# Four-quadrant products in the RWKV inverse with a loop on TensorE, and paired rope products in attention

## What is computed

```
S = S * w_t + (S a_t) b_t^T + v_t k_t^T ;  y_t = S r_t        # a = -kk, b = kk * a
y = (y - mean) * rsqrt(var + 64e-5) * ln_w + ln_b              # per head
```

```
s = (q . k) * 192**-0.5 ; s = where(kpos <= qpos, s, min) ; p = softmax(s) ; o = p v
```

## Time and profile before

| | us |
|---|---|
| median of 3 runs | 2612.54 (2611.12 to 2614.38) |
| the profiled execution's own time | 2613.09 |
| its span, first to last instruction | 2611.3 |
| PE busy | 2537.2 (97%) |
| DVE busy | 1269.4 (49%) |
| ACT busy | 862.6 (33%) |
| POOL busy | 1181.0 (45%) |

### The profile page before, as it was taken

One profiled execution on the slowest core, in us unless ns is written; L12 is line 12 of the kernel. 1 busy time (PEld: TensorE's weight loads), 2 busy tenths in 40 slices (PEclk: granted clock), 3 DMA queues, 4 the chain that ended last, 5 costly groups with the idle time before them and its releaser, 6 DMA issues.

```text
span 2611.3 us, 36164 instructions
## 1 busy us (share of the span) xinstructions
PE 2537.2 (97%) x13941; PEld 1953.8 (75%) x13941; DVE 1269.4 (49%) x1579; ACT 862.6 (33%) x1168; POOL 1181.0 (45%) x583
## 2 busy tenths in 40 slices
PE   8999999899999998889999999999999999999999
PEld 6676777688888776777788887888887446788887
DVE  7999974633322588566333223333225665433301
ACT  5432353423222344223332223322223233322321
POOL 3799844344444455113444444444443201444443
PEclk9999999899999999999999999999999999999999
DMA  5222233233323322002333233333333201333332
GB/s 148 73 73 81 73 89 91 71 89 96 95 90 91 105 74 60 4 4 77 89 96 96 86 96 93 97 96 89 93 92 87 63 25 39 91 94 91 94 94 78
DMA packets 417607, 212.85 MB, mean 82 GB/s; under 512 B 16773, under 2 KB 415931, under 8 KB 417499
## 3 DMA queue, kind: packets, MB, share of 16 engines
q1 hardware_dynamic: 414475, 209.05, 27.6%
q10 hardware_dynamic: 3024, 2.30, 0.4%
HBM read 209.22 MB, written 2.10 MB: 81 GB/s over the span
## 4 chain that ended last, share of the span: by engine, by line
PE 88%; DVE 5%; POOL 4%; ACT 2%; issue 1%; DMA 0%; ACTq 0%; DVEq 0%; POOLq 0%
PE bank L339 22%; PE bank L332 22%; PE bank L336 22%; PE bank L1330 3%; PE bank L1334 3%; PE bank L1337 3%; PE bank L2124 2%; POOL w_lo L312 1%; PE bank L2686 1%; PE bank L2685 1%; PE bank L2728 1%; PE bank L2644 1%; PE bank L2625 1%; DVE tmp L1928 1%; PE bank L2132 0%
## 5 line engine op out<-in xcount | busy, mean ns | idle before, releaser
L312 POOL TENSOR_TENSOR w_lo<-w_raw,w_hi 128x1024 fp32r<-128x1024 f32 (+3 forms) x420 | 982.1, 2339 | 1322.8 <-ACT w_hi L303 1313.4
L303 ACT ACTIVATE w_hi<-w_raw 128x1024 fp32r<-128x1024 f32 (+3 forms) x420 | 424.8, 1012 | 1369.5 <-PE bank L339 1202.2
L332 PE MATMUL bank<-hH,w_hi 128*128 128x512 f32 x1712 | 445.0, 401 | 13.9 <-ACT w_hi L303 13.0
L336 PE MATMUL bank<-hL,w_hi 128*128 128x512 f32 x1712 | 437.2, 396 | 1.6 <-DVE hL L378 1.6
L339 PE MATMUL bank<-hH,w_lo 128*128 128x512 f32 x1712 | 434.1, 395 | 0.0
L332 PEld LDWEIGHTS bank<-hH,w_hi 128*128 128x128 f32 x1712 | 322.5, 189 | 103.0 <-ACT w_hi L303 12.9
L336 PEld LDWEIGHTS bank<-hL,w_hi 128*128 128x128 f32 x1712 | 322.5, 188 | 82.4 <-DVE hL L378 3.8
L339 PEld LDWEIGHTS bank<-hH,w_lo 128*128 128x128 f32 x1712 | 320.9, 187 | 78.3
L527 DVE TENSOR_TENSOR tmp<-bank,R 128x512 f32<-128x512 f32 x88 | 60.8, 691 | 397.9 <-PE bank L339 397.7
L533 DVE TENSOR_TENSOR ffn_aL<-tmp,ffn_aH 128x512 f32 (+1 forms) x88 | 155.8, 1770 | 86.3 <-ACT ffn_aH L496 86.3
L332 PE MATMUL bank<-ffn_aH,w_hi 128*128 128x512 f32 x704 | 179.8, 395 | 0.0
(11 more groups left out here) (487 smaller groups left out, 2766.4 us busy)
## 6 DMA issues: line engine op xcount, KB each, us to landing
w_raw<-in_ffn_w_gate SPq DMA_DIRECT2D x88, 512.0 KB, 3.8
w_raw<-in_ffn_w_up SPq DMA_DIRECT2D x88, 512.0 KB, 3.8
w_raw<-in_ffn_w_down SPq DMA_DIRECT2D x64, 512.0 KB, 3.6
w_raw<-in_w_in SPq DMA_DIRECT2D x48, 512.0 KB, 3.8
w_raw<-in_even_w_in SPq DMA_DIRECT2D x26, 512.0 KB, 3.9
w_raw<-in_ffn_w_down SPq DMA_DIRECT2D x32, 384.0 KB, 3.2
w_raw<-in_w_conv_out SPq DMA_DIRECT2D x8, 512.0 KB, 3.6
w_raw<-in_w_out SPq DMA_DIRECT2D x8, 512.0 KB, 3.7
```

The costliest lines, as they stand in the source:

```text
L303: nc.scalar.activation(w_hi[u % 2][:, 0:K, :], w_raw[u % 4][:, 0:K, :], ACT.Identity).then_inc(w_hi_ready, 1)
L312: nc.gpsimd.tensor_tensor(w_lo[u % 2][:, 0:K, :], w_raw[u % 4][:, 0:K, :], w_hi[u % 2][:, 0:K, :].bitcast(F32), ALU.subtract).then_inc(w_l ...
L332: nc.tensor.matmul(out, H[:, k, :], sH[:, k0 + k, :], start=start and k == 0, stop=False)
L336: nc.tensor.matmul(out, H[:, k, :], sL[:, k0 + k, :], start=False, stop=False)
```

## The change

RWKV stage:
- A further Gram product, nt2, is nt with its output in the other half of the partitions (banks 4 and 5 in the first half, 2 and 3 in the second). dm is written into the other half too. NT and Nl come from nt2, DT straight from nt's bank by DVE, which now starts before dm.
- So D lies in the other half than DT. Sides go (rows 1 to columns 0) and (rows 0 to columns 1). Grow issues for each block D's two products and DT's two products in turn: four quadrants, two banks.
- DVE adds D of both tiles, then DT of both.
- On PE the second half's level 0 runs its sides before the group means; levels 1 to 3 are a loop with waits against the loop's register and increments of a semaphore "seen"; the gate product moves from level 1 to level 4.
- Group norm: Sqrt and reciprocal become Ln and Exp(-0.5 x) on ACT; no reciprocal on DVE.

Attention:
- The rope keys of a head fill all 128 partitions (twice 64), and odd query tiles are copied by two DMAs to the other partition half (q2).
- Per pair of tiles, first both rope products, on opposite row halves, then both plain ones. The tile order is 3, 2, 1, 0: tiles 3 and 2 before the transposes, 1 and 0 after. ACT does exps 3 and 2, both copies, then exps 1 and 0.

```diff
-        GRAMS = ["nt", "dm", "h", "rb", "rk"]
+        def d_read(w, lv, kind, e_):
+            both = lv < E_LEVELS - 1
+            return w * (4 * E_LEVELS - 2) + 4 * lv + (2 if both and kind == "dt" else 0) + e_ + 1
+        def dt_init(w, e_):
+            return 4 * w + e_ + 1
+        def d_init(w, e_):
+            return 4 * w + 2 + e_ + 1
+        GRAMS = ["nt", "nt2", "dm", "h", "rb", "rk"]
+        OTHER_HALF = ("nt2", "dm")
...
+            if name == "nt2":
+                return bank[(4 if w == 0 else 2) + i]
...
+            def group_logs(w):
+                for jj in range(2):
+                    act.wait_ge(rw["gn_ps"], 4 * w + 2 + jj + 1)
+                    s.activation(tmp[3 + jj][:, :], gn_bank(w, jj)[:, :], ACT.Ln, scale=1.0 / 64, bias=EPSG).then_inc(rw["gn_act"], 1)
             def group_roots(w):
                 for jj in range(2):
-                    act.wait_ge(rw["gn_ps"], 4 * w + 2 + jj + 1)
-                    s.activation(tmp[3 + jj][:, :], gn_bank(w, jj)[:, :], ACT.Sqrt, scale=1.0 / 64, bias=EPSG).then_inc(rw["gn_act"], 1)
+                    act.wait_ge(rw["gn_act"], 10 * w + 2 + jj + 1)
+                    s.activation(tmp[3 + jj][:, :], tmp[3 + jj][:, :], ACT.Exp, scale=-0.5).then_inc(rw["gn_act"], 1)
...
+            def inverse_start(w):
+                for jj in range(2):
+                    dt_ = b8(DTm[:, jj, :])
+                    v.wait_ge(rw["gr_ps"], gr_no(w, "nt"))
+                    V.tensor_tensor(dt_, b8(op_bank("nt", jj)[:, :]), mask_b(0), M).then_inc(dve_step, 1)
+                    v.wait_ge(dve_step, dve_sent(dve_step))
+                    V.tensor_tensor(dt_, dt_, eye_b, A).then_inc(rw["dinit"], 1)
+                    dve_sent(rw["dinit"])
             def operand_out(w, name):
+                if name == "nt":
+                    inverse_start(w)
                 for jj in range(2):
                     if name in MASKED:
                         masked_out(w, name, jj)
                     if name == "dm":
-                        inverse_start(w, jj)
+                        d_ = b8(Dm[:, jj, :])
+                        V.tensor_tensor(d_, d_, eye_b, A).then_inc(rw["dinit"], 1)
+                        v.wait_ge(rw["dinit"], dve_sent(rw["dinit"]))
...
-            def group_invert(w, jj, half):
-                r_ = tmp[3 + jj][:, 256 * half:256 * half + 256]
-                v.wait_ge(rw["gn_act"], 8 * w + 2 + jj + 1)
-                V.reciprocal(r_, r_).then_inc(dve_step, 1)
...
+                    if lv < E_LEVELS - 1:
+                        for jj in range(2):
                             v.wait_ge(rw["d_ps"], d_no(w, lv, jj) + 1)
                             V.tensor_tensor(Dm[:, jj, :], bank[4 + jj][:, :], Dm[:, jj, :], A).then_inc(rw["d_rd"], 1)
                             dve_sent(rw["d_rd"])
-                            v.wait_ge(rw["d_ps"], d_no(w, lv, jj) + 2)
-                        else:
-                            v.wait_ge(rw["d_ps"], d_no(w, lv, jj) + 1)
+                    for jj in range(2):
+                        v.wait_ge(rw["d_ps"], d_no(w, lv, jj) + (2 if lv < E_LEVELS - 1 else 1))
...
+                                half = part(1 - c if name in OTHER_HALF else c)
+                                ins = mm(op_bank(name, e_, w)[half, part(4 * (J % 2) + m_)], LEFT[name][part(e_), J, t_], RIGHT[name][part(e_), J, t_],
...
+            def inverse_sides(e_):
+                for g_ in range(NCH):
+                    for c in range(2):
+                        ins = mm(bank[e_][part(c), part(g_)], st(Nl, 1 - c, e_, g_), st(Dm, 1 - c, e_, g_), start=True, stop=True)
+                ins.then_inc(rw["m1_ps"], 1)
+            def inverse_grow(e_, both):
+                for g_ in range(NCH):
+                    if both:
+                        for c in range(2):
+                            ins_d = mm(bank[4 + e_][part(1 - c), part(g_)], st(DTm, c, e_, g_), st(M1, c, e_, g_), start=True, stop=True)
+                    for c in range(2):
+                        ins = mm(bank[6 + e_][part(c), part(g_)], st(M1, c, e_, g_), st(DTm, c, e_, g_), start=True, stop=True)
+                if both:
+                    ins_d.then_inc(rw["d_ps"], 1)
+                ins.then_inc(rw["d_ps"], 1)
...
+            FULL = E_LEVELS - 1
+            def level(w, lv, first=False, last=False, between=None, looped=False):
+                for e_ in range(2):
+                    pe.wait_ge(rw["nl"], 2 * E_LEVELS * w + 2 * lv + e_ + 1)
+                    if first:
+                        pe.wait_ge(rw["dinit"], d_init(w, e_))
+                        pe.wait_ge(rw["tr_rd"], 6 * w + 4 + e_ + 1)
+                    else:
+                        pe.wait_ge(rw["d_rd"], w * (4 * E_LEVELS - 2) + 4 * (lv - 1) + e_ + 1)
+                        if looped:
+                            pe.sem_inc(rw["seen"])
+                    inverse_sides(e_)
+                if between:
+                    between()
+                for e_ in range(2):
+                    pe.wait_ge(rw["m1_rd"], 2 * E_LEVELS * w + 2 * lv + e_ + 1)
+                    if first:
+                        pe.wait_ge(rw["dinit"], dt_init(w, e_))
+                        if w:
+                            pe.wait_ge(rw["e_rd"], e_ + 1)
+                    else:
+                        pe.wait_ge(rw["d_rd"], w * (4 * E_LEVELS - 2) + 4 * (lv - 1) + 2 + e_ + 1)
+                        if looped:
+                            pe.sem_inc(rw["seen"])
+                    inverse_grow(e_, not last)
+            def levels_first_half():
+                def fill(lv):
+                    for name in LEVEL_FILL[lv]:
+                        operand(0, name)
+                for lv in range(E_LEVELS):
+                    level(0, lv, first=lv == 0, last=lv == FULL, between=lambda: fill(lv))
+            def levels_second_half():
+                level(1, 0, first=True, between=lambda: group_means(0))
+                group_sums(0)
+                with pe.Fori(1, FULL) as lv:
+                    level(1, lv, looped=True)
+                level(1, FULL, last=True, between=lambda: group_gate(0))
...
+        kp = a.put("k_rope", [P, AH_, T])
+        q2 = a.put("q_rope_other_half", [P, 4, 2, P])
...
+        TILE_ORDER = (3, 2, 1, 0)
+        def turn_no(h, i):
+            return TT * h + TILE_ORDER.index(i) + 1
...
+                elif m_ == 15:
+                    act.wait_ge(mla["rope_t"], 4)
+                    odd_tiles = qp[:, :, :].rearrange("p h (i two c) -> p h i two c", two=2, c=P)[:, :, :, 1, :]
+                    for lo in (0, 64):
+                        act.dma_start(q2[64 - lo:P - lo, :, :, :], odd_tiles[lo:lo + 64]).then_inc(lsem, 16)
...
+            exps(0, TILE_ORDER)
             for h in range(AH_):
                 if h + 1 < AH_:
-                    exps(h + 1, range(TT - 2))
+                    exps(h + 1, TILE_ORDER[:2])
                 for part, (b_, lo_, hi_) in enumerate(((4, PTO[0], PTO[1]), (6, PTO[2], TRI[TT]))):
                     act.wait_ge(mla["t_ps"], 3 * h + (1, 3)[part])
                     if h >= 2:
                         act.wait_ge(mla["o_ps"], h - 1)
                     s.activation(probT[h % 2][:, lo_:hi_], bank[b_][:, 0:hi_ - lo_], ACT.Copy).then_inc(mla["t_act"], 1)
-                    if h + 1 < AH_:
-                        exps(h + 1, (TT - 2 + part,))
+                if h + 1 < AH_:
+                    exps(h + 1, TILE_ORDER[2:])
...
-                V.tensor_tensor(kp[r_, h // 2, :], b_[r_, :], kdup[r_, :], M).then_inc(dve_step, 1)
+                V.tensor_tensor(kp[:, h, :], b_[:, :], kdup[:, :], M).then_inc(dve_step, 1)
...
                 for i in tiles:
                     if h:
-                        pe.wait_ge(mla["exp"], TT * (h - 1) + i + 1)
-                    t_ = slice(i * P, (i + 1) * P)
+                        pe.wait_ge(mla["exp"], turn_no(h - 1, i))
+                    half = (h + i) % 2
+                    r_, n_ = slice(64 * half, 64 * half + 64), (i + 1) * P
+                    q_tile = q2[r_, h // 2, i // 2, :] if i % 2 else qp[r_, h // 2, i * P:(i + 1) * P]
+                    mm(bank[i][:, 0:n_], q_tile, kp[r_, h, 0:n_], start=True, stop=False)
+                for i in tiles:
                     n_ = (i + 1) * P
-                    mm(bank[i][:, 0:n_], qn[:, h, t_], kn[:, h, 0:n_], start=True, stop=False)
-                    mm(bank[i][:, 0:n_], qp[r_, h // 2, t_], kp[r_, h // 2, 0:n_], start=False, stop=True).then_inc(mla["s_ps"], 1)
+                    mm(bank[i][:, 0:n_], qn[:, h, i * P:(i + 1) * P], kn[:, h, 0:n_], start=False, stop=True).then_inc(mla["s_ps"], 1)
...
             for h in range(AH_):
                 if h + 1 < AH_:
-                    scores(h + 1, range(TT - 1))
+                    scores(h + 1, TILE_ORDER[:2])
...
-                    scores(h + 1, (TT - 1,))
+                    scores(h + 1, TILE_ORDER[2:])
...
```

(65 more changed lines are left out.)

59 lines of the change are left out of this document (26 added, 33 removed).

## The result

Before: 2611.83 us median (2609.09 to 2614.38, 4 runs). After: 2586.61 us (2585.69 to 2587.25, 4 runs). The ratio is 0.9905, 95% interval 0.9893 to 0.9918: 25 us or 0.95% faster. The forecast was 2594 with a range of 2582 to 2606. The profiled execution of after took 2587.25 us with a span of 2585.5.

The account below looks back on a forecast made before the run. TensorE (PE), 88% of the chain, was taken to bound the kernel, with instruction fetch a second limit. Terms +1.0 - 12.7 + 1.1 - 4.5 - 3.3 = -18.4 us gave 2594.7, stated as 2594 us, range 2582 to 2606.

Parts of the forecast that it names:

- First half and scan: First half's inverse and scan: fetch already sets the pace, the extra Gram product is mostly hidden; +1.0 us, ends -1.5 and +5.
- rival C: PE's new gaps pull its clock to 1.2 GHz; in attention +7.4 us a head, 2646 for all seven; 6%.
- Rival D: Register waits and back edges over 1 us a round, or first-half levels at low clock: +3 to +10 us; 10%.
- Second half's inverse: From group means to the a_tok product: shorter levels 0 to 4, less a loop cost; sum -12.7 us.
- Levels 2 and 3: Second half's inverse, loop rounds already in the buffer: 4.3 us each instead of 12.0 for both, -3.4 us.
- the loop's term: Second half's inverse: register waits, counter increments and two back edges cost +0.7 us, ends 0 and +3.
- level 1: Second half's inverse, the loop's first round, fetched as 1.5 blocks: 5.3 us instead of 7.7, -2.4.
- E: D and DT products take turns if two row halves in one bank exclude each other: +4.7 us, 2599; 4%.
- Products after: Products after the second half's inverse: three blocks, less fetch lead after faster levels; +1.1 us, ends 0 and +3.3.
- Tail: Output units: reciprocals leave DVE, mixH comes earlier and products after the shorter wait run faster; -4.5 us, ends -2 and -5.5.
- Attention: Seven heads: rope pairs run at once, a cycle through ScalarE's copy sets 8.8 us a head; -3.3 us, ends -1 and -9.
- rival B: Fetch has slack, 7.1 us more from first half, or attention stays on PE, 4.9 more; both 2582; 20%.

Follow-up runs that it names:

- e3: Changed kernel with levels 1 to 3 of the second half's inverse written out on TensorE instead of looped; 2590.80 us.
- e4: Changed kernel with D's sixteen products first and then DT's sixteen, instead of alternating, in both halves; 2590.26 us.
- e12: The changed kernel itself run once more, unchanged; 2587.42 us.
- e2: Only the attention part of the change, with the RWKV stage as in the kernel before; 2606.91 us, ratio to before 0.9983.
- e1: Only the RWKV part of the change, with attention as in the kernel before; 2592.59 us, ratio to before 0.9926.
- e5: Changed kernel with the group means put back ahead of level 0's sides in the second half; 2590.53 us.
- e8: Changed kernel with VectorE normalizing the next head's probabilities ahead of o_lo in attention; 2580.28 us.
- e9: Changed kernel with Sqrt on ScalarE and four VectorE reciprocal passes restored in the second half's group norm; 2593.11 us.
- e7: Changed kernel with ScalarE copying the first bank of transposed probabilities ahead of the next head's exponentials of tiles 3 and 2; 2578.93 us.
- e10: Changed kernel with both attention reorderings: ScalarE's first-bank copy ahead of the next exponentials and VectorE's normalizing ahead of o_lo; 2576.74 us.

## Why the prediction was right, point by point

Faster was given 0.88 and the median lies in the range, 7.4 us below the forecast. That the two limits (quadrants and fetch) would meet as they did is what e3 and e4 show. All misses of size but the tail's were on the fast side, so the range was hit and the sum was not: 18 us were forecast and 25 measured. Each term's own numbers, from the two profiles:

- **First half and scan: +1.0 forecast, -1.6 measured** (81.97 to 80.39 from the first Gram to the means; the repeat e12 has 78.88). The mechanism held: stalls of class issue, PE's busy time down by 7 us for 0.7. The mis-sized term is the block. I took 3.84 to 4.0 us each; the nine profiles with the change's code have 33.1 us on average for nine blocks, 3.7 each, so before's 34.56 at 33.10 busy was nearer to PE's own pace than to the fetch's. Why the scan is shorter too (37.2 on average, with nt2 in it, for 38.34) stays open. The clock looks like the reason, since before these stages were granted 0.96 and 0.93, with 0.68 in one stretch, and after 1.00. But e2 has before's code here at a higher clock, and its windows over the same two stages are longer:

```profile
1047.91:1082.69 34.78, 32.84 (x1154) 32.07 (x1154) 15.63 (x23) 7.77 (x13) 10.02 (x8) 0.98 0.02 4
1082.69:1121.89 39.20, 25.25 (x1032) 23.05 (x1028) 19.88 (x37) 6.73 (x12) 2.49 (x2) 0.98 0.02 3
```

Together that is 74.0 us, for 72.9 before. I had priced gaps as a risk to the clock (rival C and part of D); here they didn't lower it. What can be seen is that PE's wait for DVE's D just ahead of this inverse, 3.21 us before and 2.50 in e2, each followed by over 3 us at 0.50 (1047.7 to 1050.9 and 1045.7 to 1048.9), is 1.03 us in after, with no such stretch.
- **Second half's inverse: -12.7 forecast, -14.1 measured.** Level 0 -6.0 (forecast -6.2), level 4 -1.4 (-1.4). Levels 2 and 3 took 8.55 us where 8.6 and 0.7 for the loop were forecast, so the loop's term isn't seen on top of the rounds. The other step that was mis-sized is level 1, 5.3 forecast and 4.52 measured: the means and the sums ahead of it are sixteen products that take 4 us, time in which the fetch can get ahead (argued, not tested by itself; the round was 5.06 in e1 and 5.60 in e5). The rows of idle time that can be put down to the loop are 0.27 and 0.25 us, one at each back edge. Rival D is out, E too: e4 shows what D and DT in turn would cost, and level 0's grow calls are what is left of its 5.86 us after means and sums of 1.98 each, 1.9 us for 128 records.
- **Products after: +1.1 forecast, -0.7 measured.** The fetch stall is there (1.64 us of issue at 1155.64), but the stage runs at 1.00 where it had 0.91. Here the clock does show: with the same code e1 and e8 were granted 0.85 and 0.83 in it and took 20.19 and 19.99 us, after and e12 1.00 and took 19.13 and 19.16.
- **Tail: -4.5 forecast, -3.7 measured** (34.17 to 30.49). The 2.75 us of waiting became 1.03, and the unit of eight now waits 1.04 us for ScalarE's w_hi, which before was ready. That second wait is the step that I left out: ScalarE, not PE, carries the residual's passes between the short units. e9 gives the reciprocals a price of 4.7 us, low clock included, against a tail that has to load the root's table.
- **Attention: -3.3 forecast, -4.4 measured** between the two profiles (84.91 to 80.49). The head period was forecast at 8.8 and is 8.69, 0.4 below before, six times: -2.3. The first head's part, 20.01 to 18.20, gave -1.8 instead of -1.0. The rest, -0.3, is in the last head, where both profiles show the low clock (0.84 and 0.83 over it). The cycle was the bound, and PE wasn't: e7, e8 and e10 take it apart and find 7.48 us under it. The "8.1 us of work" of rival B was too high by 0.6; with 7.48 against the measured 8.69, its other side would have been 1.2 x 7 = 8.5 us, not 4.9.
- The remaining 1.4 us lies ahead of the first Gram product, in code that the change doesn't touch, inside the scatter of 2.7.

Of the rivals, B's half on fetch is answered by e4 (no slack), and C didn't happen: attention shows 1.00 in all but the last head.

## What to carry to other kernels

Before making a stream of small products faster, count its instructions in blocks of 256 and look how far apart idle rows of class issue stand: where blocks arrive every 3.7 to 4.0 us and their products need less, a faster order buys nothing, and a loop saves the fetch of its repeats less the time that they still run. Fill a known wait with work that is ready, for the wait's clock as well as its time. And when one engine waits a little in each turn of a cycle, look at the order of work on the *others*: moving one copy ahead of two exponentials on ScalarE gave 7.7 us on top of the change (e7), more than its whole attention part had given (4.9 us, e2).

## What the hardware showed that was not expected

- Blocks of 256 PE instructions arrive 3.96 to 3.99 us apart when nothing else stalls the stream (e3), 3.4 to 4.0 in the first half. The stall can fall in the middle of a call. A loop body of 384 matmul and load instructions ran its third round with no packet on q8.
- 128 records on four quadrants took 1.9 us with both row halves writing each of the two banks (D and DT, level 0), the rate of the Gram calls, where each bank is written from one row half (64 in 1.14 us with the drain).
- A wait of 2.76 us on the way into the means came with a granted clock of 0.50 in all three profiles that have it (before, e2, e5), one of 2.81 us in attention was followed by 0.50 in eight profiles of eleven, and the gaps of up to 1.6 us in the first half's inverse left it at 1.00 in after and in e12.
- Busy time hides waits: 7.94 us "busy" in a head were 7.48 once every operand came early.
